# Two-block transformer kernel: modulation rows turned by transposes, residual squares added on VectorE before one sum, per-head sums as two fp32r products

## The reference

```python
def first_block(x, ...):
    for i in range(DEPTH):
        hn = _rmsnorm(x, norm_mix[i])
        if i % 2 == 0: x = x + _gated_deltanet(hn, ...)
        else:          x = x + _dilated_attention(hn, ...)
        x = x + _swiglu(_rmsnorm(x, norm_ffn[i]), ffn_w_in[i], ffn_w_out[i])

def _rmsnorm(x, w):
    return x * rsqrt(mean(x * x, -1) + 1e-6) * w

def _dilated_attention(h, w_in, q_norm, k_norm, w_out):
    qkv = (h @ w_in).reshape(b, s, 3, 3, 8, 64)    # 24 heads of 64 for q, k and v
    q, k, v = _rmsnorm(qkv[:, :, 0], q_norm), _rmsnorm(qkv[:, :, 1], k_norm), qkv[:, :, 2]
    ...

def second_block(x, c, ctx, c_ctx, w_mod, b_mod, ...):
    for l in range(DEPTH):
        mod = split_cols(silu(c) @ w_mod[l] + b_mod[l], 6)        # and the same for c_ctx
        ...   # the scales sc1 and sc2 are used as 1 + scale
```

## Time and profile before

| | |
|---|---|
| median of 3 runs | 3567.61 us (3564.16 to 3568.55) |
| profiled execution, first to last instruction (span) | 3562.6 us |
| PE, DVE, ACT, POOL busy | 95%, 45%, 33%, 9% |
| gdn out-projection to its root | about 440 to 503 us |
| dilated q and k pieces | about 883 to 1042 us |
| dilated attention steps with modulation | about 1112 to 1225 us |
| dil out-projection to its root | about 1238 to 1272 us |

### The profile page before, as it was taken

The page is one execution under the profiler, slowest core; times in us unless marked ns, Lnnn a source line. Parts: engine busy times, 40 slices in busy tenths (PEclk is TensorE's granted clock), DMA queues, the critical chain, the costliest instruction groups (busy, mean ns, idle before and its releaser), DMA issues.

```text
span 3562.6 us, 42226 instructions
## 1 busy us (share of the span) xinstructions
PE 3383.0 (95%) x17826; PEld 2768.8 (78%) x17826; DVE 1600.9 (45%) x2730; ACT 1163.6 (33%) x1982; POOL 303.8 (9%) x545
## 2 busy tenths in 40 slices
PE   7999989999999899999999998999999989989999
PEld 5887868887778778886877676888887777767886
DVE  5747534444323454454226544434434325545443
ACT  6446322122433332222235433311112225532222
POOL 1101000000000000001000011300001301012000
PEclk9999999999999899999999898999999899999999
DMA  3111022322226224222214322221021112022420
GB/s 129 48 38 58 20 76 71 118 95 83 74 81 237 86 83 142 71 71 84 68 66 151 128 85 71 71 71 47 26 70 66 40 48 98 1 71 71 142 71 36
DMA packets 190542, 281.97 MB, mean 79 GB/s; under 512 B 18952, under 2 KB 121864, under 8 KB 190224
## 3 DMA queue, kind: packets, MB, share of 16 engines
q1 hardware_dynamic: 188176, 272.19, 22.5%
q10 hardware_dynamic: 2176, 7.08, 0.6%
HBM read 274.01 MB, written 2.10 MB: 77 GB/s over the span
## 4 chain that ended last, share of the span: by engine, by line
PE 89%; ACT 4%; DVE 3%; POOL 2%; issue 1%; DMA 1%; SPq 1%; ACTq 0%; POOLq 0%; DVEq 0%
PE ps L750 10%; PE ps L752 10%; PE ps L751 10%; PE ps L498 6%; PE ps L499 6%; PE ps L500 6%; PE ps L781 5%; PE ps L782 5%; PE ps L783 5%; PE ps L394 4%; PE ps L388 3%; PE ps L1323 3%; PE ps L414 2%; PE ps L566 2%; PE ps L567 2%; PE ps L568 2%
## 5 line engine op out<-in xcount | busy, mean ns | idle before, releaser
L403 ACT ACTIVATE R<-ring 128x1024 fp32r<-128x1024 f32 (+4 forms) x285 | 402.1, 1418 | 1042.1 <-PE ps L752 346.3
L750 PE MATMUL ps<-R,R 128*128 128x512 f32 (+1 forms) x1760 | 654.2, 372 | 16.9 <-DVE R L444 9.8
L751 PE MATMUL ps<-R,R 128*128 128x512 f32 (+1 forms) x1760 | 650.9, 370 | 0.0
L752 PE MATMUL ps<-R,R 128*128 128x512 f32 (+1 forms) x1760 | 650.8, 370 | 0.0
L498 PE MATMUL ps<-R,R 128*128 128x512 f32 (+1 forms) x1016 | 420.0, 413 | 34.5 <-DVE R L444 11.6
L750 PEld LDWEIGHTS ps<-R,R 128*128 128x128 f32 x1760 | 334.5, 190 | 79.7 <-DVE R L444 11.4
L499 PE MATMUL ps<-R,R 128*128 128x512 f32 (+1 forms) x1016 | 388.9, 383 | 0.0
L500 PE MATMUL ps<-R,ringlo 128*128 128x512 f32 (+1 forms) x1016 | 388.0, 382 | 0.0
L752 PEld LDWEIGHTS ps<-R,R 128*128 128x128 f32 x1760 | 334.1, 190 | 56.0
L751 PEld LDWEIGHTS ps<-R,R 128*128 128x128 f32 x1760 | 334.6, 190 | 54.8
L688 DVE TENSOR_TENSOR R<-ring,R 128x2048 fp32r<-128x2048 f32 x88 | 203.6, 2317 | 309.7 <-ACT R L403 309.7
(11 more groups left out here) (273 smaller groups left out, 4698.4 us busy)
## 6 DMA issues: line engine op xcount, KB each, us to landing
ring<-in_w_mod SPq DMA_DIRECT2D x24, 2048.0 KB, 8.0
ring<-in_ffn_w_in SPq DMA_DIRECT2D x44, 1024.0 KB, 11.9
ring<-in_w_ffn_in SPq DMA_DIRECT2D x44, 1024.0 KB, 12.2
ring<-in_ffn_w_out SPq DMA_DIRECT2D x10, 2048.0 KB, 7.9
ring<-in_w_ffn_out SPq DMA_DIRECT2D x10, 2048.0 KB, 7.8
ring<-in_dil_w_in SPq DMA_DIRECT2D x9, 2048.0 KB, 7.7
ring<-in_gdn_w_in SPq DMA_DIRECT2D x8, 2048.0 KB, 8.6
ring<-in_w_o SPq DMA_DIRECT2D x6, 2048.0 KB, 8.4
```

The costliest lines, as they stand in the source:

```text
L403: return act.e.activation(o, i, fn, **kw)
L750: pe.e.matmul(ps, w[0], x[0], start=(k == 0), stop=False)
L751: pe.e.matmul(ps, w[0], x[1], start=False, stop=False)
L752: t = pe.e.matmul(ps, w[1], x[0], start=False, stop=(k == 7))
```

## The change

Three edits. (1) In add_x, ScalarE writes the square of block 0 to a buffer `total` (part of Z, or DI), VectorE adds the squares of blocks 1 to 6 to it one by one, each behind the next block's addition to X, and TensorE multiplies only twice, behind the last piece: ones by total, ones by the square of block 7. (2) In head_norm, GpSimd rounds the squares to fp32r (hi), VectorE subtracts (lo), and TensorE makes two fp32r products with an fp32r copy of bones, BONES, in place of one float32 product. (3) The modulation row is turned by four transposes, each 128 by 128, and VectorE adds the four row groups (a reduction) and then the bias and the 1 in one instruction.

```diff
@@ -321,7 +321,6 @@
         ident = KC[:, K_ID:K_ID + 128]
         ones = KC[:, K_ONE:K_ONE + 128]
         bones = KC[:, K_BONE:K_BONE + 128]
-        by_vector = KC[:, K_SEL:K_SEL + 2]
         by_sum = KC[:, K_SUM:K_SUM + 6]
         e1, e64, ea2, one1, e128 = (KC[:, K_EPS + n:K_EPS + n + 1] for n in range(5))
 
@@ -603,8 +602,8 @@
                 elif what == "evac" and p.evac.dve:
                     p.evac.dve(n, s, PS.of(*product_name(p, n, s)), product_name(p, n, s))
 
-        def pool_products(pieces):
-            for what, p, n, s in steps(pieces):
+        def pool_products(pieces, lead=1):
+            for what, p, n, s in steps(pieces, lead):
                 if what == "evac" and p.evac.pool:
                     p.evac.pool(n, s, PS.of(*product_name(p, n, s)), product_name(p, n, s))
 
@@ -615,20 +614,36 @@
             dve.wait_ge(*at(*name))
             dve.e.tensor_tensor(X[:, n, :], X[:, n, :], ps, A_).then_inc(*dve.done("ps", *name))
 
-        def add_x(tag, act_too={}, dve_too={}):
+        def add_x(tag, total, act_too={}, dve_too={}):
 
             def on_pe(n, s, ps, name):
-                pe_square(n, 8, S, ones, tag)
+                if n < 7:
+                    return
+                ps = bank(tag)
+                pe.wait_ge(*at("sq read", tag, 6))
+                pe.e.matmul(ps, ones, total, start=True, stop=False)
+                pe.wait_ge(*at("square", tag, 7))
+                pe.e.matmul(ps, ones, SQ.of(tag, 7)[:, 0:S], start=False, stop=True).then_inc(*pe.done("sq read", tag, 7))
+                pe.mark("sum", tag)
 
             def on_act(n, s, ps, name):
                 act.wait_ge(*at("x", tag, n))
-                act_square(X[:, n, :], S, tag, n)
+                if n:
+                    act_square(X[:, n, :], S, tag, n)
+                else:
+                    activate(total, X[:, 0, :], ACT.Square).then_inc(*act.done("square", tag, 0))
                 if n in act_too:
                     act_too[n]()
 
             def on_dve(n, s, ps, name):
                 dve_add_x(n, s, ps, name)
                 dve.mark("x", tag, n)
+                if n > 1:
+                    dve.wait_ge(*at("square", tag, n - 1))
+                    if n > 2:
+                        dve.wait_ge(*at("sq read", tag, n - 2))
+                    dve.e.tensor_tensor(total, total, SQ.of(tag, n - 1)[:, 0:S], A_).then_inc(
+                        *dve.done("sq read", tag, n - 1))
                 if n in dve_too:
                     dve_too[n]()
             return Evac(pe=on_pe, act=on_act, dve=on_dve)
@@ -1449,10 +1464,8 @@
                 return
             ps = bank("mod", l, c, "turn")
             pe.wait_ge(*at("mod row", l, c))
-            for j in range(4):
-                t = pe.e.matmul(ps[:, 2 * j:2 * j + 2], mod_row(l)[:, j * 128:(j + 1) * 128], by_vector, start=True,
-                                stop=True)
-            t.then_inc(*pe.done("mod turned", l, c))
+            tp([(ps[:, j * 128:(j + 1) * 128], mod_row(l)[:, j * 128:(j + 1) * 128]) for j in range(4)]).then_inc(
+                *pe.done("mod turned", l, c))
 
         def dve_mod(l, c, half):
             if half == 0:
@@ -1465,12 +1478,12 @@
             dve.wait_ge(*at("mod turned", l, c))
             o = C_BMOD + 48 * l + 4 * c
             z = MODS[l][:, 4 * c:4 * c + 4, :]
-            dve.e.tensor_tensor(z, PS.of("mod", l, c, "turn")[:, 0:8].rearrange("p (a b) -> p a b", b=2),
-                                COL[:, o:o + 4].unsqueeze(2).broadcast_to([128, 4, 2]), A_).then_inc(
-                *dve.done("ps", "mod", l, c, "turn"))
-            if c in (2, 3, 8, 9):
-                dve.wait_ge(*at("ps", "mod", l, c, "turn"))
-                dve.e.tensor_scalar(z, z, 1.0, None, A_).then_inc(*dve.done("mod one", l, c))
+            groups = PS.of("mod", l, c, "turn").rearrange("p (j g r) -> p j r g", j=4, g=4)[:, :, 0:2, :]
+            dve.e.tensor_reduce(z, groups, AX, A_).then_inc(*dve.done("ps", "mod", l, c, "turn"))
+            dve.wait_ge(*at("ps", "mod", l, c, "turn"))
+            dve.e.scalar_tensor_tensor(z, z, 1.0 if c in (2, 3, 8, 9) else 0.0,
+                                       COL[:, o:o + 4].unsqueeze(2).broadcast_to([128, 4, 2]), A_, A_).then_inc(
+                *dve.done("mod there", l, c))
 
         def mods_at(step, first=0):
 
@@ -2084,7 +2097,7 @@
 
         def pool_gdn(hg):
             gdn_ready(pool, hg)
-            pool_products(qkv_pieces(hg))
+            pool_products(qkv_pieces(hg), 2 - hg)
             pool_heads(hg, 12)
 
 
@@ -2094,7 +2107,7 @@
         WHGO = new_ring([ru(o, 1024) for o in (4096 + bufs[7], 4096 + bufs[7] + 1024, UX)])
 
         def gdn_out_pieces():
-            return columns("gdn out w", 0, 1024, 8, [o_gdn], add_x("ffn 0", {5: lambda: act_ffn_w_in("ffn 0", 0)},
+            return columns("gdn out w", 0, 1024, 8, [o_gdn], add_x("ffn 0", Z[:, 0, :], {5: lambda: act_ffn_w_in("ffn 0", 0)},
                                                                    {5: lambda: dve_ffn_w_in("ffn 0", 0)}))
 
         def sp_gdn_out():
@@ -2142,22 +2155,41 @@
         WHD = wh_ring(UX)
         wd = a["dil_w_in"]
 
+        BONES = ru(29952, 128)
+        SPLIT = new_ring([(ru(27904 + 1024 * i, 512), ru(28416 + 1024 * i, 512)) for i in range(2)])
+
         def head_norm(dst, g, scale, eps):
 
             def on_pe(n, s, ps, name):
-                pe_squares(1, 512, bones, "head", name)
+                ps = bank("head", name)
+                hi, lo = SPLIT.of("head", name)
+                pe.wait_ge(*at("head ones"))
+                pe.wait_ge(*at("sq read", "head", name, 0))
+                pe.e.matmul(ps, BONES, hi, start=True, stop=False)
+                pe.e.matmul(ps, BONES, lo, start=False, stop=True).then_inc(*pe.done("sum", "head", name))
 
             def on_act(n, s, ps, name):
                 act.wait_ge(*at(*name))
                 act_square(ps, 512, "head", name, 0)
                 act_rstd(512, scale, eps, "head", name)
 
+            def on_pool(n, s, ps, name):
+                (hi, lo), before = SPLIT.take("head", name)
+                pool.wait_ge(*at("square", "head", name, 0))
+                if before:
+                    pool.wait_ge(*at("sum", *before))
+                pool.e.tensor_copy(hi, SQ.of("head", name, 0)[:, :]).then_inc(*pool.done("square hi", "head", name))
+
             def on_dve(n, s, ps, name):
+                hi, lo = SPLIT.of("head", name)
+                dve.wait_ge(*at("square hi", "head", name))
+                dve.e.tensor_tensor(lo, SQ.of("head", name, 0)[:, :], hi, SUB).then_inc(
+                    *dve.done("sq read", "head", name, 0))
                 dve.wait_ge(*at("rstd", "head", name))
                 dve.e.scalar_tensor_tensor(dst[:, n, :], ps, g, RR.of("head", name)[:, :], M, M).then_inc(
                     *dve.done("ps", *name))
                 dve.mark("rr read", "head", name)
-            return Evac(pe=on_pe, act=on_act, dve=on_dve)
+            return Evac(pe=on_pe, act=on_act, dve=on_dve, pool=on_pool)
 
         def store_vd(c):
             def on_act(n, s, ps, name):
@@ -2438,6 +2470,8 @@
         def pool_dil():
             pool.wait_ge(*at("end", "ffn 0", "pe"))
             pool_parts("h dil", d_hi, d_src, (0, 2, 4, 6), ("h", "rms dil"))
+            pool.e.tensor_copy(BONES, bones).then_inc(*pool.done("head ones"))
+            pool_products(dil_pieces(), 2)
             pool.wait_ge(*at("dil out", 7))
             for z in range(2):
                 pool.wait_ge(*at("dil weights", z))
@@ -2463,7 +2497,7 @@
         WHDO = wh_ring(UX)
 
         def dil_out_pieces():
-            return columns("dil out w", 0, 1024, 4, [o_dil], add_x("ffn 1", {5: lambda: act_ffn_w_in("ffn 1", 0)},
+            return columns("dil out w", 0, 1024, 4, [o_dil], add_x("ffn 1", DI, {5: lambda: act_ffn_w_in("ffn 1", 0)},
                                                                    {5: lambda: dve_ffn_w_in("ffn 1", 0)}))
 
         def sp_dil_out():
```

## The result

The changed kernel takes 3527.2 us (median of 4 runs, 3525.7 to 3529.62) where the kernel before, beside it on the same chip, takes 3568.1 (4 runs, 3564.16 to 3570.33): a ratio of 0.9886, 95% interval 0.9872 to 0.99. That is 40.9 us less, where 19.3 were forecast. The profiled execution has a span of 3523.9 us, 38.7 less than before. An execution that is listed with its span is 1.8 to 1.9 us longer than it; of the 5.0 us between the span and the median of the kernel before, the rest was the distance of a quick profiled execution from the median.

A forecast was written before the change was run, and what follows sets the result against it. TensorE, 89% of the chain, was taken as the bound. Terms -10.0 - 4.0 - 5.3 + 0 = -19.3 us take the span from 3562.6 to 3543.3, median 3548.3; own range 3545 to 3552, wider range 3541 to 3558.

The forecast's parts named there:

- edit 3: Modulation turn: transposes cost TensorE about what selection products do, and VectorE's additions fit beside its wait; taken as 0 us.
- a selection product that was cheaper than a transpose in the mixing stage: Mixing stage's modulation turn: named as one of two things that would make the forecast wrong; no size given.
- Edit 1, gdn out: First out-projection: sums between products, the wait before the first and the slow stretch behind it go; -10.0 us.
- Edit 1, dil out: Dilated out-projection: last square and additions finish earlier, but the two sums may run at 1.2 GHz; -4.0 us.
- Edit 2: Dilated q and k head sums: 0.41 us less per piece, -10.0 over 24, and +4.7 at the ends; -5.3 us.
- terms of the ends: First and last head sums: cast and subtraction uncovered, +1.5 each, and +1.7 for a slow clock behind the first; +4.7 us.
- Late lo: q and k head sums: GpSimd's cast is blocked in each piece and TensorE waits; +5 us, 3553; chance 0.13.
- Clock kept: TensorE stays at 2.4 GHz where 1.7 and 1.2 were charged, and the cast takes 0.61; -4, 3544; chance 0.12.
- The feed-forward gives it back: Before the feed-forward: the out-projections' 14 us gain is lost because second weights come no earlier; 3562, no change; chance 0.04.
- Slower: q and k pieces: GpSimd's cast and the subtraction set the pace; a loss of 9 us (3577) at 7.30; chance 0.03.

The follow-up runs named there:

- e8: The changed kernel with the four two-column selection products put back before the transposes, their result overwritten: 3546.0 us, 18.4 us more than the changed kernel.
- e1: The kernel before with only the modulation turn by transposes and VectorE's reduction: 3545.3 us, against 3566.4 for the kernel before.
- e2: The changed kernel with the modulation turn put back to two-column selection products: 3551.4 us, 0.9959 of the kernel before.
- e9: The kernel before with only the residual squares added on VectorE and two float32 sums: 3556.0 us, against 3567.6 for the kernel before.
- e10: The kernel before with only the head sums made as two fp32r products: 3563.2 us, 0.9992 of the kernel before.
- e3: The changed kernel with selection products back in place of transposes, each widened from 2 to 128 columns: 3532.8 us, 0.9911 of the kernel before.
- e7: The changed kernel with selection products back in place of transposes, each widened from 2 to 32 columns: 3531.4 us, 0.9918 of the kernel before.
- e11: The changed kernel with one two-column selection product per turn instead of transposes, three quarters of modulation values left out: 3519.5 us, 0.9872 of the kernel before.
- e6: The changed kernel with the first and last of 24 head sums as one float32 product again: 3522.2 us, against 3527.5 for the changed kernel.

## Why the prediction was wrong

The direction was right, and the time was outside the range because of one step: **edit 3, for which I took 0**. The prediction read "the eight records of selection products take 1.00 us and eight of a turn by L394, the new operation, 1.09" and saw no difference. Two things were wrong with it.

- *The unit.* A float32 product leaves two records, a float32 transpose one. The eight selection records are one turn; the eight of L394 are two groups of four transposes. A turn costs 0.53 us against 0.93, 0.40 less, and 24 of them 9.6; without the clock the two stages are 2.0 and 3.5 us shorter in these two traces, 5.5 and not 9.6. In e8, where the spare products cost 18.4 us and not 22.3, a part is hidden as well; what hides it was not looked into. Over all traces with a full turn, the attention stage is 107.5 to 109.4 us with selection products and 104.3 to 106.0 with transposes alone. The row that would have told was there: 992 records of L394 can be counted against the program.
- *The clock.* I looked for slow stretches only behind waits. The mixing stage had five, 22.1 us lost, and three of them, 15.3 us, came with TensorE busy throughout. With edit 3 the two at waits were left, 6.8 us. The 15.3 us are the largest term of the whole change. e1, e2, e9 and e10 show that this gain comes with edit 3 and with nothing else; e3, e7 and e11 that it comes without any transpose. What the chip weighs there is left open beyond these forms. The prediction's last part named "a selection product that was cheaper than a transpose in the mixing stage" as a danger: the right place with the wrong sign. Edit 3 alone measured -21.1 us, which is what the forecast of -19.3 lacks to the measured -40.9. The 3.2 us that the attention stage's clock also gave in these two traces can't be put down to it, since that loss varies with and without edit 3.

The other steps, by their own terms:

- **Edit 1, gdn out**: -10.0 forecast, -8.8 measured. From head end (457.7) to table load 36.9 us, as worked out, without a wait behind the first pieces and at clock 1.00. The 1.1 us are missing because the head itself ended later; in e10, without edit 1, it also did (461.62 - 3.67 = 457.95, 456.57 before), so it is no cost of the edit. Both have the clock of 0.72 from 440 to 452, where the kernel before and e9, with edit 1 alone, have 0.86; e9's table load starts at 492.9, 10.5 earlier than before. In the trace of the changed kernel the slow stretch ahead of the place was longer by about what edit 1 took away.
- **Edit 1, dil out**: -4.0 forecast, 28.77 - 25.19 = -3.6 measured. To the sums 21.4 us (21.5 forecast); the two sums took 3.82 where I had 2.02 and 1.2 for the clock. Edit 1 alone measured -11.7 by medians against -14.0.
- **Edit 2**: -5.3 forecast. First to last sum, 1026.93 - 891.60 = 135.33 us instead of 142.58, and 1.98 more at the first: -5.3. Alone it measured -4.5 by medians, with an interval that holds 0. The terms of the ends (+4.7) are borne out by e6, which takes them back, less 0.4 for each of two sums, and gains 5.3 where 3.5 to 4 were expected; one part was missed, the longer slow stretch behind the last sum. It is the 1.1 us that the next stage loses in the table, and -5.3 and +1.1 make -4.2, near e10's -4.5.
- **Rivals.** *Late lo*: no, the middle sums don't wait, though the cast takes 1.19 us beside L585. *Clock kept*: no for both places. *The feed-forward gives it back*: no, the first product behind gdn out starts at 500.05 instead of 508.88. *Slower*: no.

## What to carry to other kernels

Count what one operation leaves in the trace before taking its price from a group: products and transposes of the same operands leave different numbers of records. Read the granted clock of every stretch in which TensorE is busy, not only behind its waits: products with hardly any columns can cost more in the clock of a stage than in their own time (here 15.3 us against some 12 x 0.93 = 11 in the mixing stage), and widening them to columns nobody needs can make a kernel faster (here by some 19 us). When a split shortens a sum but lengthens its chain, use it only where a product covers the chain; at the ends, where TensorE waits, the slow single product is the better one.

## What was not expected of the hardware

- Same instructions, 32 columns instead of 2: the mixing stage takes 194.8 us instead of 210.0. The stage's clock loss takes just two values over twelve traces, 6.8 (to 0.1) and 22.1 or 22.2 us; the four traces at 22 are all of the slower group of executions.
- Transposes did not harm the clock. The Trainium skill, page "TensorE: Matmul & The Clock Gate", section "Part 4: PE-mode transpose", says that the full clock does not engage in transpose mode. If L393 runs in that mode (the kernel calls `pe.e.transpose`, the trace's record says only MATMUL), putting transposes for products should have left the mixing stage at 0.89 or lower; it went to 0.96, and the measurement decides.
- The clock behind a wait is not fixed by the wait: 3.66 us of idle time were followed by a loss of 1.7 us in one execution, 3.67 in another by almost none, where a longer slow stretch had come before (e10). Likewise the attention stage lost 3.9 to 9.1 us in different traces, with and without edit 3.
